# Decode of a hybrid attention step: four value buffers in place of two

## The reference, cut to what matters

```python
ka = jnp.concatenate([ck_a.astype(ak.dtype), ak], axis=1)
va = jnp.concatenate([cv_a.astype(av.dtype), av], axis=1)
...
for w, d in A_PATTERNS:
    o, lse = gather_attention(aq, ka, va, rel_bias[:, :A_HEADS], d, w // d, buf_a)
    outs.append(o)
    lses.append(lse)
o_a = combine_by_denominator(outs, lses)
o_b, lse_b = gather_attention(bq, kb, vb, rel_bias[:, A_HEADS:], 1, B_WINDOW, buf_b)
o_b = o_b * jax.nn.sigmoid(lse_b - sink_l.astype(jnp.float32))[..., None]
```

## Time and profile before

| | |
|---|---|
| median of 3 runs | 2813.31 us (2811.78 to 2815.5) |
| the profiled execution: its own time | 2814.37 us |
| its span in the profile | 2812.6 us |
| TensorE busy over the span | 2611.2 us (93%) |
| GpSimd busy over the span | 1124.5 us (40%) |
| mean rate of the DMA engines over the span | 141 GB/s |

### The profile page before, as it was taken

How to read it: one execution, slowest core, us unless ns; L and a number is a source line. 1 busy time by engine, 2 the same in 40 slices (tenths; PEclk the granted TensorE clock), 3 DMA queues, 4 the chain that set the end, 5 groups by cost and what they waited for, 6 DMA issues and landing times.

```text
span 2812.6 us, 34922 instructions
## 1 busy us (share of the span) xinstructions
PE 2611.2 (93%) x13959; PEld 2255.9 (80%) x13959; DVE 697.4 (25%) x1648; ACT 985.6 (35%) x1685; POOL 1124.5 (40%) x677
## 2 busy tenths in 40 slices
PE   6999999789997948994999999999999999999997
PEld 4899999789995527773888887888878888988985
DVE  5421011066663235551101012010120101201102
ACT  4211221077774525552423324233242332421321
POOL 4200000057762312211645546455464564543641
PEclk8999999989998979997999999999999999999998
DMA  4311312199957946666444545445454464322222
GB/s 136 111 38 56 128 58 77 61 175 186 173 91 196 255 134 180 193 185 189 141 149 135 199 158 182 145 139 200 151 186 151 128 252 143 129 89 79 87 89 69
DMA packets 299831, 395.31 MB, mean 141 GB/s; under 512 B 81306, under 2 KB 233290, under 8 KB 295014
## 3 DMA queue, kind: packets, MB, share of 16 engines
q1 hardware_dynamic: 285968, 302.02, 38.1%
q10 hardware_dynamic: 7078, 70.34, 7.0%
q0 software_dynamic: 6624, 20.72, 2.7%
HBM read 327.68 MB, written 121.05 MB: 160 GB/s over the span
## 4 chain that ended last, share of the span: by engine, by line
PE 50%; DMA 2%; issue 1%; DVE 1%; ACT 0%; POOL 0%; SPq 0%; ACTq 0%; DVEq 0%
PE ml_y L1727 25%; PE ml_up L1698 8%; PE ml_up L1699 8%; PE ml_up L1700 8%; DMA ml_x<-scratch_x 1%; DMA ml_raw<-in_w_up 1%; PE ml_y L1722 1%; PE ml_y L1721 0%; DVE ml_a L1829 0%; DVE ml_y L1867 0%; DVE ml_y L1871 0%; ACT ml_square L1776 0%; POOL ml_w_lo L1659 0%; ACT ml_r L1756 0%; ACT ml_a_hi L1762 0%
## 5 line engine op out<-in xcount | busy, mean ns | idle before, releaser
L1659 POOL TENSOR_TENSOR ml_w_lo<-ml_raw,ml_w_hi 128x1024 fp32r<-128x1024 f32 x256 | 613.7, 2398 | 480.8 <-ACT ml_w_hi L1747 480.8
L1698 PE MATMUL ml_up<-ml_h_hi,ml_w_hi 128*128 128x512 f32 (+1 forms) x1280 | 453.1, 354 | 39.7 <-POOL ml_w_lo L1659 28.0
L1747 ACT CAST ml_w_hi<-ml_raw 128x1024 fp32r<-128x1024 f32 x256 | 268.1, 1048 | 589.4 <-PE ml_y L1727 401.6
L1700 PE MATMUL ml_up<-ml_h_hi,ml_w_lo 128*128 128x512 f32 (+1 forms) x1280 | 452.6, 354 | 0.0
L1699 PE MATMUL ml_up<-ml_h_lo,ml_w_hi 128*128 128x512 f32 (+1 forms) x1280 | 452.3, 353 | 0.0
L1727 PE MATMUL ml_y<-ml_w_hi,ml_a_hi 128*128 128x512 f32 x1024 | 398.5, 389 | 0.0
L1727 PE MATMUL ml_y<-ml_w_lo,ml_a_hi 128*128 128x512 f32 x1024 | 398.4, 389 | 0.0
L1727 PE MATMUL ml_y<-ml_w_hi,ml_a_lo 128*128 128x512 f32 x1024 | 398.3, 389 | 0.0
L1698 PEld LDWEIGHTS ml_up<-ml_h_hi,ml_w_hi 128*128 128x128 f32 x1280 | 242.4, 189 | 73.0 <-POOL ml_w_lo L1659 28.2
L386 PE MATMUL pj_acc<-pj_h_hi,pj_w_hi 128*128 128x424 f32 (+1 forms) x800 | 289.6, 362 | 1.0 <-DVE pj_h_lo L580 1.0
L387 PE MATMUL pj_acc<-pj_h_lo,pj_w_hi 128*128 128x424 f32 (+1 forms) x800 | 285.4, 357 | 0.0
(11 more groups left out here) (212 smaller groups left out, 3633.2 us busy)
## 6 DMA issues: line engine op xcount, KB each, us to landing
ml_raw<-in_w_up SPq DMA_DIRECT2D x64, 1024.0 KB
ml_raw<-in_w_down SPq DMA_DIRECT2D x64, 1024.0 KB
out_o_a_k_s<-in_cache_a_k ACTq DMA_DIRECT2D x8, 3060.0 KB, 12.2
out_o_a_v_s<-in_cache_a_v ACTq DMA_DIRECT2D x8, 3060.0 KB, 12.7
at_raw<-scratch_pt SPq DMA_DIRECT2D x36, 512.0 KB, 7.8
scratch_pt<-pj_proj SPq DMA_DIRECT2D x10, 1056.0 KB, 4.1
pj_w<-in_w_in SPq DMA_DIRECT2D x20, 512.0 KB, 3.9
op_part<-scratch_part SPq DMA_DIRECT2D x16, 594.0 KB, 6.3
```

Of the source, the lines that this page charges most:

```text
L1659: nc.gpsimd.tensor_tensor(split_of(w_lo, n), raw_of(n), f32(split_of(w_hi, n)), ALU.subtract).then_inc(w_lo_ready, 1)
L1698: pe.matmul(out, hi[:, k, :], h_hi[:, k, cols], start=(k == 0), stop=False)
L1700: last = pe.matmul(out, lo[:, k, :], h_hi[:, k, cols], start=False, stop=(k == DBLK - 1))
L1747: nc.scalar.copy(split_of(w_hi, n), raw_of(n)).then_inc(w_hi_ready, 1)
```

## The change

The value tiles `v` and `v_new` get four buffers in place of two, with a semaphore for each. Sequence b uses buffer b % 4. Values of b >= 4 wait for `weigh(b - 4)`; those of sequences 0 to 3 are issued with no wait. The loads are the same, in the same order, through the same queue. The memset of `v_new` covers twice the elements (4 x 512 a partition in place of 2 x 512). Keys, and everything that TensorE does, stay as they are.

```diff
--- before.py
+++ after.py
@@ -1978,14 +1978,14 @@
     CHUNK_SIDE = (LEFT, RIGHT, RIGHT, LEFT)
     CHUNK_BANK = (0, 0, 1, 1)
     SCORED_AT = (5, 6, 10, 7)
-    KEYS, TURNED = 6, 3
+    KEYS, TURNED, VALUES = 6, 3, 4
     TILE_B, TILE_NEW = KT, KT + 1
 
     with Phase(nc, "de") as ph:
         ident = keep.ident
         q_all = ph.sb("q_all", [P, DEC_B, 4, DEC_T, AH])
-        v = ph.sb("v", [P, 2, V_COLS])
-        v_new = ph.sb("v_new", [P, 2, AW + KVW])
+        v = ph.sb("v", [P, VALUES, V_COLS])
+        v_new = ph.sb("v_new", [P, VALUES, AW + KVW])
         k_t = ph.sb("k_t", [P, KEYS, 512])
         prob = ph.sb("prob", [QH, 2, A_KEYS + B_KEYS + 1])
         low = ph.sb("low", [QH, 2, CHUNKS])
@@ -2005,8 +2005,8 @@
         zeroed = ph.sem("zeroed")
         q_zeroed = ph.sem("q_zeroed")
         q_placed = ph.sem("q_placed")
-        v_in = ph.sems("v_in", 2)
-        v_new_in = ph.sems("v_new_in", 2)
+        v_in = ph.sems("v_in", VALUES)
+        v_new_in = ph.sems("v_new_in", VALUES)
         kt_ready = ph.sem("kt_ready")
         kt_copied = ph.sem("kt_copied")
         scored = ph.sem("scored")
@@ -2049,11 +2049,11 @@
             nc.gpsimd.memset(total[:], 1.0).then_inc(zeroed, 1)
 
             def load_values(b):
-                s = b % 2
+                s = b % VALUES
                 flat = d["cache_a_v"].rearrange("l b t h e -> (l b) t (h e)")[b]
                 new = d["kv"][SEQ:, :].rearrange("(b t) c -> b t c", t=DEC_T)[b]
-                if b >= 2:
-                    pool.wait_ge(weighed, 2 * (b - 1))
+                if b >= VALUES:
+                    pool.wait_ge(weighed, 2 * (b - VALUES + 1))
                 tiles = v[:, s, 0:KT * AW].rearrange("p (t c) -> p t c", c=AW)
                 for t in range(FAR_T):
                     far = flat[t * 2 * P:(t + 1) * 2 * P, :].rearrange("(g r) c -> g r c", r=16)[:, 0:DEC_T, :]
@@ -2118,11 +2118,11 @@
                              ident[0:QH, 0:QH]).then_inc(pt_ready, 1)
 
             def weigh(b):
-                s = b % 2
+                s = b % VALUES
                 if b == 0:
                     pe.wait_ge(zeroed, ZEROED)
-                pe.wait_ge(v_in[s], 16 * (FAR_T + 2) * (b // 2 + 1))
-                pe.wait_ge(v_new_in[s], 32 * (b // 2 + 1))
+                pe.wait_ge(v_in[s], 16 * (FAR_T + 2) * (b // VALUES + 1))
+                pe.wait_ge(v_new_in[s], 32 * (b // VALUES + 1))
                 pe.wait_ge(pt_copied, 3 * (b + 1))
                 if b:
                     pe.wait_ge(o_masked, 3 * b)
```

## The result

The changed kernel takes 2825.8 us (median of 5 runs, 2821.65 to 2830.22) against 2813.87 us for the kernel before (5 runs, 2811.78 to 2821.48). The ratio is 1.004, with a 95% interval from 1.0021 to 1.0059: slower by 6 to 17 us. The forecast was 2826.2, in a range of 2822.5 to 2830.

The account below looks back on a forecast made before the run. Decode was taken to sit on two nearly equal limits per step, TensorE's 14.92 us and the DMA engines' 15.07. Terms 8.0 + 2.2 + 3.5 + 0.45 - 1.25 = 12.9 us later gave 2826.2 us, range 2822.5 to 2830.

Parts of the forecast that it names:

- S2: Moment TensorE begins the keys of sequence 2; forecast 8.0 us later, as early values share the DMA engines by packet.
- slow start of step 2: TensorE's step on sequence 2: the new wait before it lowers the clock, costing 2.2 us.
- wait before K3: TensorE waits 3.5 us for the keys of sequence 3, which finish only with the values of sequence 4.
- steps 3 to 6 over four of 14.92: Later decode steps: three run at the DMA engines' 15.07 us against TensorE's 14.92, adding 0.45 us.
- K7's wait, gone: The present wait before the keys of sequence 7, 1.25 us, disappears.
- S7: Moment TensorE begins the keys of sequence 7; forecast at 990.0 against 977.11, 12.9 us later.
- The memset: First memset of decode: 0.85 us longer, so values of sequence 0 start later and keys of sequence 1 gain 1.7 us.
- "up" bound: Decode's upper bound, +16.8 us: another clock loss of 2.2 at sequence 3's keys, and steps at the slowest engine's rate.
- the pace of the slowest engine: Upper-bound case for the later steps: each takes 15.65 us, three of them adding 1.7 us.
- K2 alone is late: Rival: keys of sequence 2 are late but those of sequence 3 are not; 9.0 us slower, 2822; chance 0.09.
- Equal bytes: Rival: the two load queues share the DMA engines by bytes, not packets; no change, 2815 to 2817 us; chance 0.09.
- hidden anyway: Rival: keys of sequence 2 and all later keys land in time; 5.2 us faster, 2808; chance 0.06, hidden or slightly faster.

Follow-up runs that it names:

- four_old_waits: The changed kernel's four value buffers, but values of sequence 2 on still wait as in the kernel before: 2817.56 us, ratio 1.0014 to the kernel before.
- swapped_four: The changed kernel, four value buffers, with queues swapped: GpSimd issues the keys, SyncE the values; 2810.68 us, ratio 0.9977 to the kernel before.
- one_queue_four: The changed kernel's four value buffers, all values issued through SyncE's queue, each behind the keys needed before it: 2813.97 us, ratio 0.9985 to the kernel before.
- three_buffers: The changed kernel with three value buffers in place of four, so only the values of sequence 2 go early: 2825.15 us, ratio 1.0036 to the kernel before.
- early_two_only: The changed kernel, values of sequences 2 and 3 sent without a wait, later ones waiting as before the change: 2825.09 us, ratio 1.0037 to the kernel before.
- four_old_look: Second profiled execution of four_old_waits, the same code run alone: 2811.64 us.
- swapped_two: The kernel before, two value buffers, with queues swapped: GpSimd issues the keys, SyncE the values; 2810.21 us, ratio 0.9977 to the kernel before.

## Why the prediction was right

**The direction and the cause.** Values were not late, keys were just in time, and the engines had no room: all three held. four_old_waits shows that the buffers without early values don't bring the loss, swapped_four that early values on the queue with the small packets don't either, and one_queue_four that the order repairs it. Packet turns were forecast to share as in the earlier trace rows; 915 to 917 packets confirm it, and the swap turns the shares round.

**The terms.** How much later than in the first profile of before (us):

| | forecast | first profile | second profile |
|---|---|---|---|
| S2 | 8.0 | 7.23 | 10.58 |
| slow start of step 2 (its length less its wait and 14.92) | 2.2 | 2.85 | 2.26 |
| wait before K3 | 3.5 | 2.21 | 3.65 |
| steps 3 to 6 over four of 14.92 | 0.45 | 0.58 | 1.59 |
| K7's wait, gone | -1.25 | -1.25 | -1.25 |
| S7 | 12.9 | 11.62 | 16.83 |

The large terms have the right sign and the right order of size. Decode ended 11.2 and 16.6 us later, and the medians differ by 11.9.

**How much was luck.** The forecast of 2826.2 against 2825.8 is closer than the method can be. Two profiles of the changed kernel lie 5 us apart, the interval of the measured difference is 6 to 17 us, and the forecast was made from one profile. What the runs bear out is the range and the mechanism, not the last microsecond.

**K2.** S2 was forecast at 43.5 us after the first memset; 42.7 and 46.1 were measured. The wait before it was larger than forecast in the first profile (13.9 against 9.7), since TensorE was ready 5.0 us sooner. K1 came 2.8 us earlier than forecast (14.6 against 17.4). And step 1 did not pay its slow start of 2.2 us, which the prediction had it pay "now and again afterwards": after the short wait of 2.0 us its 16 transposes took 2.07 us. Neither moved the sum, because K2's bytes and not TensorE set S2. In the second profile step 1 did pay, and the wait was 10.6 us.

**The memset.** It shifts V0 by 0.9 us (first memset to V0's issue 2.8 before, 3.7 after), as forecast. The 1.7 us for K1 are not shown. K1 was reached at 14.6 to 19.5 us in the five profiles with the memset of four buffers and the old queues, 16.8 in the mean, and at 19.1 and 18.5 in those of the kernel before: that points the right way, but the spread is larger than the term.

**The clock.** With no wait behind it, step 2 took 17.5 us in three_buffers and 16.4 in early_two_only, so the slow start cost 2.6 and 1.5 there. The 16 transposes after the wait took 3.67 us in the change, as in the earlier trace rows.

**K3.** S3 was forecast at 64.1; 62.7 and 66.9 were measured. Neither early_two_only, where V4 goes late, nor three_buffers has a wait there.

**The later steps.** In both profiles the excess is all in step 3, and every step from S4 on takes 14.91 or 14.92 us. In the first it is the wait of 0.53 us before K4. In the second it is the slow start after the wait of 3.65 us, a case that the "up" bound of the forecast had at 2.2. So the three steps at the pace of the DMA engines, 15.07 us, were not seen, and the agreement of 0.58 with 0.45 is chance; nor was the pace of the slowest engine.

**The rivals.** "K2 alone is late" (2822) leaves out V4. Its time lies inside the measured interval, so the times can't refuse it; the waits before K3 in both profiles, which go away when V4 is held back, do. "Equal bytes" and "hidden anyway" are refused by S2. That the queue doesn't hold four loads is refused as well: V0 to V3 went out in one go, by 889.5 us.

**Left open.** Why K1 lands anywhere from 14.6 to 19.5 us in executions of the same code, and whether two more buffers cost some 0.1% by themselves where the order is the old one.

## What to carry to other kernels

More buffers make transfers start earlier; ask first what else is on the engines at that moment, and whether it is needed sooner. Where DMA time for a step is about equal to compute time, a prefetch is a change of order and no gain: find the load that is waited for, and see that nothing stands beside it. Which queue issues what matters as much as when: here the queue with the larger packets took the larger part of the shared engines (0.199 MB/us against 0.084), so the urgent load belongs on it.

## What the runs showed of the hardware

Where both load queues were full, they took turns packet for packet in the kernel before (481 to 473) and in the change (915 to 917). With the queues swapped it was only roughly so, 629 packets of GpSimd's queue to 711 of SyncE's. The share in bytes follows the packet size: 2.9 to 3.1 KB from GpSimd's queue against 1.3 KB from SyncE's for tiles of the same shape. All through SyncE's queue, the 16 engines moved 245 to 256 GB/s from 900 us on, at a share of 1.09 to 1.10, against 272 with the mix; but from 880 to 890 us the one queue moved 2.81 MB, 281 GB/s, so the packet size alone doesn't explain the lower rate.

SyncE itself was held up at issuing. In the changed kernel six transfers of K3 took it 10.36 us, where they took 3.76 before, and a small one behind them 10.32. Columns are start, us, and the transfer; the last row is K3's in the kernel before.

```profile
886.18 10.36 SPq L1964 DMA_DIRECT2D dk_k<-in_cache_a_k  x6
896.58 1.71 SPq L1965 DMA_DIRECT2D dk_k<-in_cache_a_k  x1
...
898.89 10.32 SPq L1967 DMA_DIRECT2D dk_k_new<-scratch_kv  x1
909.25 0.30 SPq L1968 DMA_DIRECT2D dk_k_new<-scratch_kv  x1
```

```profile
895.06 3.76 SPq L1964 DMA_DIRECT2D dk_k<-in_cache_a_k  x6
```

All four profiles with early values behind SyncE's keys have this small transfer at 10.1 to 10.8 us, and it ends 1.7 to 3.0 us after TensorE began K2. So here a queue whose packets drained slowly also held up the engine that feeds it. GpSimd showed no such hold with four loads of values queued. K3's last transfer was issued by 909.55, 16.7 us before TensorE began K3, and from 892 to 906 the keys' queue moved its packets one for one with the values', so the hold is not what K3 waited for; in a kernel where SyncE issues other loads too, it could be a second cost.

How much a wait cost of the clock differed between waits of nearly the same length. After 3.25 us (K2 in four_old_look) the 16 transposes took 1.99 us, after 3.65 (K3 in the second profile of the change) 2.86, and after 3.72 (K1 in swapped_two) 3.67. The granted clock over these transposes, by stretch, in the same order:

```profile
898.36:900.35 1.99, 1.99 (x18) 1.78 (x20) 0.00 (x0) 1.30 (x3) 1.99 (x4) 1.00 1.09 276
```

```profile
931.92:934.78 2.86, 2.86 (x18) 2.53 (x20) 0.00 (x0) 1.67 (x3) 2.25 (x4) 0.66 1.12 272
```

```profile
879.19:882.86 3.67, 3.67 (x18) 3.34 (x20) 0.00 (x0) 1.76 (x3) 0.68 (x2) 0.50 1.07 279
```

1.00 is TensorE at its upper level, 0.50 at the lower one, and 0.66 a stretch with part of each.
